# The buffers of the split weights begin at 64 modulo 128 instead of 0

## The reference, cut to what matters

```python
u = rmsnorm(x, g) @ w_in                    # 2048 x 12288, split into ten parts
ya = b_g * causal_dwconv3(c_g * xa) * silu(za)
yb = hgrn2(q, k, v, log_f) * silu(og)       # 8 heads of 128
m = sigmoid(ga) * (ya @ w_a) + sigmoid(gb) * (yb @ w_b)
x = x + m @ w_o
x = x + sigmoid(rmsnorm(x) @ w_gate) * (p @ w_proj)
# second block, on rmsnorm(x)
h = rms_norm(x, g) * (1 + scale) + shift    # scale, shift, gate = silu(c) @ w_ada + b_ada
q_a, k_a, v_a, z_a, q_r, k_r, v_r, z_r = split(h @ w_in2)
y = concat(dilated_attention(...) * silu(z_a), retention(...) * silu(z_r))
out = rms_norm(x + gate * (y @ w_out2))
```

## Time and profile before

| | us |
|---|---|
| median of three runs | 2576.95 (2576.51 to 2577.50) |
| the profiled execution, its own time | 2576.79 |
| its span, first to last instruction | 2575.5 |
| TensorE busy | 2561.5 |
| VectorE busy | 1311.2 |
| ScalarE busy | 923.1 |

### The profile page before, as it was taken

How to read it: one execution, slowest core, us unless ns; L and a number is a source line. 1 busy time by engine, 2 the same in 40 slices (tenths; PEclk the granted TensorE clock), 3 DMA queues, 4 the chain that set the end, 5 groups by cost and what they waited for, 6 DMA issues and landing times.

```text
span 2575.5 us, 31606 instructions
## 1 busy us (share of the span) xinstructions
PE 2561.5 (99%) x13068; PEld 2109.4 (82%) x13068; DVE 1311.2 (51%) x2101; ACT 923.1 (36%) x1294; POOL 79.0 (3%) x64
## 2 busy tenths in 40 slices
PE   9999999999999999999999999999999999999998
PEld 8887788877888888888888888778888888888888
DVE  7557634468334555655442363363355545554425
ACT  6543325343223222322232353332344334444423
POOL 0000000000000000000000102100000000000000
PEclk9999999999999999999999999999999999999999
DMA  5322233322334666666442232235322222222424
GB/s 195 106 83 74 83 98 99 90 75 79 94 98 142 216 215 216 220 209 211 140 166 104 90 107 94 86 106 165 90 66 82 82 80 77 82 82 82 163 99 156
DMA packets 159984, 309.29 MB, mean 120 GB/s; under 512 B 11040, under 2 KB 15392, under 8 KB 158816
## 3 DMA queue, kind: packets, MB, share of 16 engines
q1 hardware_dynamic: 159040, 305.70, 36.8%
q0 software_dynamic: 224, 1.15, 0.1%
q10 hardware_dynamic: 576, 0.42, 0.1%
HBM read 298.84 MB, written 8.39 MB: 119 GB/s over the span
## 4 chain that ended last, share of the span: by engine, by line
PE 98%; DVE 1%; issue 0%; ACT 0%; DVEq 0%; ACTq 0%
PE bank L339 92%; PE bank L1213 1%; PE bank L1214 1%; PE bank L1215 1%; PE bank L770 1%; PE bank L415 1%; PE bank L718 1%; PE bank L1373 1%; PE bank L1547 0%; DVE CGB L2009 0%; PE bank L726 0%; DVE X L1938 0%; PE bank L740 0%; PE bank L1650 0%; PE bank L741 0%
## 5 line engine op out<-in xcount | busy, mean ns | idle before, releaser
L339 PE MATMUL bank<-XH,WH 128*128 128x512 f32 (+1 forms) x2880 | 1115.5, 390 | 1.6 <-issue 1.6
L339 PE MATMUL bank<-XH,WL 128*128 128x512 f32 (+1 forms) x2880 | 1102.9, 385 | 0.0
L339 PE MATMUL bank<-XL,WH 128*128 128x512 f32 (+1 forms) x2880 | 1102.8, 385 | 0.0
L389 DVE TENSOR_TENSOR WL<-RAW,WH 128x1024 fp32r<-128x1024 f32 x443 | 543.0, 1227 | 898.4 <-ACT WH L366 897.6
L366 ACT CAST WH<-RAW 128x1024 fp32r<-128x1024 f32 x443 | 463.8, 1048 | 1105.8 <-PE bank L339 1102.0
L339 PEld LDWEIGHTS bank<-XH,WH 128*128 128x128 f32 x2880 | 540.9, 188 | 112.1 <-issue 5.3
L339 PEld LDWEIGHTS bank<-XL,WH 128*128 128x128 f32 x2880 | 541.1, 188 | 109.0 <-issue 2.9
L339 PEld LDWEIGHTS bank<-XH,WL 128*128 128x128 f32 x2880 | 540.8, 188 | 108.9 <-DVE WL L389 0.3
L339 PE MATMUL bank<-WH,XH 128*128 128x512 f32 x384 | 150.6, 392 | 0.0
L339 PE MATMUL bank<-WH,XL 128*128 128x512 f32 x384 | 149.6, 390 | 0.0
L339 PE MATMUL bank<-WL,XH 128*128 128x512 f32 x384 | 149.6, 390 | 0.0
(11 more groups left out here) (293 smaller groups left out, 1757.8 us busy)
## 6 DMA issues: line engine op xcount, KB each, us to landing
RAW<-in_w_in SPq DMA_DIRECT2D x303, 512.0 KB, 3.6
AST<-in_w_ada SPq DMA_DIRECT2D x192, 256.0 KB, 4.0
RAW<-in_w_out SPq DMA_DIRECT2D x40, 512.0 KB, 3.5
RAW<-in_w_o SPq DMA_DIRECT2D x32, 512.0 KB, 3.4
RAW<-in_w_gate SPq DMA_DIRECT2D x32, 512.0 KB, 3.4
RAW<-in_w_a SPq DMA_DIRECT2D x16, 512.0 KB, 4.2
RAW<-in_w_b SPq DMA_DIRECT2D x16, 512.0 KB, 4.2
XT<-in_xT SPq DMA_DIRECT2D x4, 1024.0 KB, 7.6
```

What stands on the lines that cost most here:

```text
L339: ins = nc.tensor.matmul(bank[b][:, cols], l, r[:, cols], start=first, stop=final)
L389: nc.vector.tensor_tensor(WL[:, m % NSPL], RAW[:, m % NRAW], WH[:, m % NSPL].bitcast(F32), ALU.subtract).then_inc(lo.sem, lo.step(m))
```

## The change: 64 bytes for the weights, 128 for what follows

`WH` and `WL` begin 64 bytes later. `XH`, `XL`, `C0` and with it `W0` and all tensors that are placed by them begin 128 bytes later, as does the scratch `SC`, which is placed by the offset of `XL`. `RAW` stays. Between the end of `WL` and the start of `XH` 64 bytes are unused. No instruction, shape or wait is touched.

```diff
     RAW = sb("RAW", [NRAW, 2, 512], F32, 0)
-    WH = sb("WH", [NSPL, 2, 512], F32R, 16384)
-    WL = sb("WL", [NSPL, 2, 512], F32R, 28672)
-    XH = sb("XH", [16, 512], F32R, 40960)
-    XL = sb("XL", [16, 512], F32R, 73728)
-    C0 = 106496
+    WH = sb("WH", [NSPL, 2, 512], F32R, 16384 + 64)
+    WL = sb("WL", [NSPL, 2, 512], F32R, 28672 + 64)
+    XH = sb("XH", [16, 512], F32R, 41088)
+    XL = sb("XL", [16, 512], F32R, 73856)
+    C0 = 106624
@@
-    SC = sb("SC", [5, 512], F32, 73728 + 11 * 2048)
+    SC = sb("SC", [5, 512], F32, 73856 + 11 * 2048)
```

## The result

| | before | after |
|---|---|---|
| median, us | 2577.20 (2576.51 to 2577.50, four runs) | 2600.05 (2599.91 to 2600.22, four runs) |
| ratio, 95% interval | | 1.0088 (1.0076 to 1.0101) |
| span of the profiled execution, us | 2575.5 | 2598.8 |
| TensorE busy, us | 2561.5 | 2585.6 |

The change makes the kernel slower by 0.9%, 22.9 us. The prediction was wrong: it had forecast 2577 us, with a range that ended at 2590, and had given the slower side 0.14. In what follows, d is the address at which the streamed tensor starts less the address at which the loaded (stationary) one starts, modulo 256. A "pace" is the mean distance from one start to the next over all matmuls of a kind; distances of 250 ns or more, where something stands between two of them, are left out.

The account below looks back on a forecast made before the run. The prediction took TensorE, busy for 99% of the span, and the pace of its matmuls to bound the kernel. Every term was zero, so the median of 2576.95 us gave a forecast of 2577.0 us, range 2565 to 2590.

Parts of the forecast that it names:

- the slower side: Outcome for the whole kernel: slower by over 0.2%, given a chance of 0.14.
- the parts on the other engines: ScalarE's conversion (L366) and VectorE's subtraction (L389): zero change, within 4 ns of 1048 and 1227 ns, off the path.
- a distance of 64 between weights and stream: TensorE's stream against its weight load: no row shows this distance; put at zero by the nearest row.
- The products with w_a: TensorE matmuls streaming YH and YL, said to start at 32 against weights at 0: 227 ns, as with both at 0.
- The value products: Retention's matmuls (L1213 to L1215), said to load slices from 32 that straddle five lines: 226.4 ns, so zero for the load.
- every other tensor keeps its residue: Tensors other than WH and WL move by 128 bytes, so addresses modulo 128 stay; zero, with 1 us either way.
- A collision is dodged: Rival, TensorE: load and stream meet in memory, and a distance of 64 frees it; 2565 to 2461 us, chance 0.14.
- the 13 ns at each change of the weights: TensorE: fixed price per matmul, 227 ns less 2 x 107 for the columns, the same at 512 and 256 columns.
- The price of 216 ns: Float32 products with ones need 216 ns per weight change and as many columns; so up to 116 us could go.
- The fifth line costs: Rival, TensorE's weight load: a slice over five 128-byte lines loads a quarter longer; 2584 us, or 2619; chance 0.14.
- It doesn't do what it says: Rival: the allocator rounds the start, so addresses stay as they were; 2577 us, sharing 0.72 with the forecast.
- The rivals' large forms: The full collision, 2461 us, and the full fifth line, 2619 us; left out of the range, 0.07 on each side.

Follow-up runs that it names:

- e1: Against the kernel before, WH and WL stay; XH, XL, C0 and what follows move by 128 bytes: 2629.89 us, 1.0205.
- e6: The kernel before with QH moved to the place of the scratch words SS, at KH's residue, and SS moved elsewhere: 2575.03 us, 0.9991.
- e2: Against the kernel before, WH, WL, XH, XL and C0 all move alike by 64 bytes: 2577.25 us, 1.0002.
- s1_sweep: All computation left out, zeros written; 44 cases of 96 dense matmuls back to back, each with its own starts: 226.7 ns at equal starts.
- e4: Against the kernel before, WH and WL move by 64 bytes and all that follows by 256: 2635.41 us, 1.0225.
- s3_distance: All computation left out; distances between starts in steps of 16 bytes, TensorE emptied ahead of each case: 226.7 ns at 0, 228.9 at 64.
- s4_fine: All computation left out, TensorE emptied ahead of each case; distances in steps of 4 bytes without the multiples of 16: 227.1 to 240.0 ns.

## Why the prediction was wrong, point by point

**The place was right.** TensorE is full, nothing makes it wait, and only the pace of the matmuls can move the end: that held to the digit. So did the parts on the other engines, at 1047 and 1227 ns. The mark set for being wrong, a pace at 512 columns that moves by more than 0.5 ns, is what happened: 2.0 ns dense and 6.3 swapped. The one part that was named as shown by no row, a distance of 64 between weights and stream, is the part that cost. This is the term of the sum that was wrong: it was put at zero "by the nearest row" and measured 24.3 us by the paces (2.0 ns on 8256 matmuls, 2.2 on 768 and 6.3 on the 1152 swapped ones, where the sign is the other way, less 2.2 on 384).

**The row that it was put at zero by wasn't one: a sum of residues failed.** The prediction, and the comment beside `W0` in the excerpt of the kernel ahead of it, take `NVEC` to be 176. It is 168, the sum of the widths in the kernel's list of vectors. So `W0` = `C0` + 3680 + 672 = `C0` + 17 x 256, and `YH`, `XH1`, `TR` and `VR` started at the very residue of `WH` and `XH`, not 32 beyond; `XX`, `TMP` and `R0` stood at 32 modulo 128, not 64. With that, the two bounds fall. The products with w_a were no evidence on a distance of 32: they stood at distance 0. The value products were none on slices that straddle a line: they didn't. "Distances of 0 and 32 cost the same" had no row at all, and in the sweep 32 costs 6.6 ns. The evidence agreed so well with the forecast because it was the same case three times over. The right residues would have left the zero without any row; whether the forecast would then have been another, nothing shows.

**The modulus was taken for granted.** Only residues modulo 128 were worked out, so "every other tensor keeps its residue" hid that the distance between `XH` and unmoved weights would go from 0 to 128 modulo 256. That half, put at nothing in the sum, is e1's 53 us.

**The row that showed the effect was in the trace.** One split tensor stood off the others, `QH`, and only the score products of retention and attention use it: at d = 64 where it streams, at -64 where it is loaded. Retention's are on the last row and the next two. The groups of L1213 to L1215 in before show attention's apart (xcount, busy us, mean ns):

```profile
L1213 PE MATMUL bank<-KH,QH 128*128 128x512 f32 x32 | 12.7, 398 | 0.0
...
L1214 PE MATMUL bank<-PL,TR 128*128 128x512 f32 x32 | 12.5, 389 | 0.0
```

398 ns for the product with `QH` and 389 for one without, both with no idle time ahead of them. In e6 both have 389. A mean from the list of groups doesn't give the pace, as the prediction says, but of two groups of one shape the longer one calls for reading its starts, and the starts of retention's three show 237 ns each, 10 more than the dense ones. Priced from there, with up to 10 ns on 10,176 matmuls, the slower side would have had a rival of up to 100 us, and its chance wouldn't have been 0.14.

**The rivals.** *A collision is dodged*: no start that was tried gave less than 226.67 at 512 columns. Nearly all distances other than 0 add to the 13 ns at each change of the weights, and none takes anything off them; what they are, no run shows. The price of 216 ns was taken from another type, and none of the starts tried comes near it. At 256 columns the sign was right: 117.8 instead of 120.0, 0.8 us in all. *The fifth line costs*: the sign was right and the mechanism wrong, by e2; that 128 bytes are a unit of the load at all was supposed, and no run shows it. *It doesn't do what it says*: the addresses did move, or nothing could have changed.
By the rule of the Trainium skill's page "SBUF — State Buffer" (Who interferes with whom), weights and stream come through two independent ports and TensorE waits on nobody. As far as other engines go the traces still agree (229.6 and 228.9 ns in the two stretches above, which one matmul more or less at an edge would even out, with VectorE busy for 58.2 of 90 us and for 46.9 of 130 us); between load and stream they don't: 226.7 ns at d = 0 and 232.4 at d = 128 differ in nothing but where the two start.

**What the chances lacked.** The range was built from two mechanisms that were imagined, each with a small price, where the honest bound for a distance that no row shows was the spread between groups of one shape in the trace. The rivals' large forms were given 0.07 each; the measured time lies 10 us past the end of the range.

## What to carry to other kernels

Where TensorE loads new float32r weights for every matmul of 512 columns, start stationary and streamed tensors at the same residue modulo 256, and move them by multiples of 256 together. Work residues out from the numbers that the program really uses, print them, and keep the modulus open: of a bound that rests on "this row stands at another residue", the residue is to be proved first. When one group of a shape is longer than its siblings with no idle time ahead of it, look at its starts before it is put aside.

## What was unexpected of the hardware

- The pace of float32r matmuls with a weight load each depends on the distance of the two starts modulo 256, and hardly on where either starts: 226.7 ns at 0, 228.9 at 64, 232.4 at 128, 233.3 at 192, up to 240.0 at 20 (512 columns). At 384 columns the four gave 173.3, 173.3, 176.0 and 174.7; at 256, 120.0, 113.3, 120.0 and 117.8; at 128 all four 111.7.
- One distance can have more than one settled pace. At d = 64 these are 228.9 and 233.3 at 512 columns (s1_sweep; the swapped groups of e4) and 113.3 and 117.8 at 256, where -64 shows the same two in e4. At 512 columns d = 112 gave 226.7 in s3_distance and 231.1 in s1_sweep, and 240 (the starts 16 and 0, weights first) gave 233.3 and 226.7. Emptying TensorE doesn't decide it: with the starts 0 and 64 and TensorE emptied, 256 columns settled at 113.3 in s3_distance and at 117.8 in s4_fine. What does decide stays open.
- In the change's dense products the steps go round in threes, 232, 226 and 229 ns, and after a disturbance the round starts at another of the three operands. Together with the five slow matmuls behind the score products this says that the state reaches over several matmuls.
- Why 256 bytes, and which part of the chip meets which, stays open. What a type other than float32r does wasn't tried.
